# The first channel quarter's modulation in two halves, in one core's hybrid decoder layer

## The chip, the core and the metric

The kernel runs on one core of a Trainium2 chip. The metric is the device time of one execution in microseconds (us), here the median of three runs. The engines are PE (TensorE matmuls), PEld (its weight loads), DVE (VectorE), ACT (ScalarE), POOL (GpSimd) and SP (SyncE, which issues the large loads). Each works through its own program in order, and semaphores tie them together.

## What is computed

One step of a hybrid decoder layer for 256 prompt rows and 32 sample rows (8 sequences of 4), 288 rows in all, D_MODEL = 2048, all in float32.

```
mods = silu(c) @ w_ada + b_ada          # -> shift1, scale1, gate1, shift2, scale2, gate2
h    = RMSNorm(x; g_pre1) * (1 + scale1) + shift1
h @ w_in -> q, k, v, forget logits, u, B, C, gA, gB
A    = forgetting attention(q, k, v)    # 16 heads x 64
y    = B * conv3_causal(C * u)
m    = (sigmoid(gA) * (A @ w_oa) + sigmoid(gB) * (y @ w_ob)) @ w_o
x    = x + gate1 * RMSNorm(m; g_post1)
x    = x + gate2 * RMSNorm(SwiGLU(RMSNorm(x; g_pre2) * (1 + scale2) + shift2); g_post2)
```

There are 9 conditioning rows: one for the prompt, 8 for the samples. `w_ada` is 2048 x 12288.

## The kernel before

**Layout and precision.** Activations lie transposed: 16 tiles of 128 channels, each with 288 columns (`NT`). Every float32 product of weights and activations is three matmuls in the fast 32-bit format: the weights are split into `w_hi` (ACT, a cast) and `w_lo` (DVE, `raw - w_hi`), the activations into `a_hi` and `a_lo`. One load into `raw` brings 4 channel tiles (`SK`) by 512 weight columns (`SN`), 1 MiB. There are 4 `raw` buffers (`RAW`) and 2 split buffers (`SPLIT`). `product` multiplies one load: for each of 4 column tiles of 128 (`mt`, one PSUM bank each) it runs 4 channel tiles x 3 matmuls, 48 in all.

**Rounds.** The first stage computes u, C and B. It goes channel quarter by channel quarter (4 channel tiles each), so that it can start before the whole of h is there. A quarter has five rounds, one for each of five groups of 512 columns (`CUT` = 5, `round_cols`). Round n has column group n % 5 and quarter n // 5; there are 20. In quarter 0 ACT copies the result out of the banks into `acc_half` (`first_round`), in later quarters DVE adds it there (`later_round`). A round can use a bank only when its previous content is out (`bank_turn`), and its split buffer only when the round two before it is multiplied (`mm_turn`).

**Visits.** scale1 and shift1 of a channel quarter are 512 columns of `w_ada` each. One visit brings one of them: four loads of 1 MiB, one per quarter of the summed dimension, into the ring `ada`, then `ada_slot` for each (4 matmuls of 128 x 512 float32 in four column strips of PE, into bank 4), a copy to `ada_sb` (ACT, `copy_ada`), four transposes into bank 5 (PE, `ada_transpose`), and a reduction into `mods` (DVE, `add_ada`). Visit 2c is the scale of quarter c, visit 2c + 1 its shift. A slot of the ring is loaded again when the visit before has multiplied it (`ada_turn`). Visits 0 and 1 stand before round 0, visit 2 behind round 1, visit 3 behind round 3, 4 and 5 behind rounds 5 and 7, 6 and 7 behind rounds 10 and 12. The transposes of a visit stand inside the round behind it, between two column tiles (`between`).

**From a visit to h.** Behind the scale: `prepare_scale` (DVE: bias, `modA`, x * scale * rstd into `xn`). Behind the shift: `prepare_shift` (DVE), `split_h` (ACT: `a_hi`, in two pieces of 2 channel tiles), `h_lo` (DVE: `a_lo`, likewise). A quarter's first round waits for its `h_lo` (`act_lo`).

**Order.** The order on every engine is written out by hand. SP issues the loads of rounds and visits in one fixed sequence (`load_first`, `load_rounds`), and each issue waits until its buffer is free. While SP waits, all loads behind it in its program wait too. Fillers (`keep_warm`: matmuls of 256 columns whose result is not used) stand in the lead-in where PE would have nothing to do.

## Time and profile before

| | |
|---|---|
| median of 3 runs | 1842.09 us |
| lowest, highest | 1840.67, 1842.49 us |
| the profiled execution's own time | 1839.91 us |
| its span, first to last instruction | 1838.1 us |
| PE busy in the span | 1806.4 us, 98% |
| PE, first product of round 0 | 44.57 us |
| PE, first product of quarter 1 | 86.93 us |
| DVE busy, ACT busy | 875.1 us (48%), 704.8 us (38%) |

The page of the profile gives busy times, the costliest groups of instructions by line, and what ended the idle time before them. The timeline merges instructions of one line that follow one another on an engine; an instruction's end there is its result, so the next one often starts before it. "x32" of a visit's matmuls stands for 16 instructions in two records each. SPq rows are the issues of loads, and an issue lasts as long as the queue has no room. The time to landing is counted from the issue.

### The profile page before, as it was taken

The page shows a single profiled execution, that of the slowest core. Times are in us where ns is not written, and L with a number is a line of the kernel's source. Part 1 is how long each engine was busy: PE and PEld are TensorE (multiplying, and loading weights), DVE is VectorE, ACT ScalarE, POOL GpSimd, SP SyncE. Part 2 cuts the span into 40 slices and gives each one's busy share as a digit, 9 for nine tenths or more (in the row PEclk, how much of TensorE's full clock was granted, in tenths as well). Part 3 has the DMA queues.
Part 4 walks back from the last instruction along what each step waited for, and adds up shares of the span by engine and source line. Part 5 has one row for each costly group of instructions (what it writes and reads, how often), then busy time and mean ns, then how long its engine had stood idle before and what let it go on. Part 6 is the DMA issues. An engine that isn't in the chain of part 4 may idle for free.

```text
span 1838.1 us, 31832 instructions
## 1 busy us (share of the span) xinstructions
PE 1806.4 (98%) x13703; PEld 1684.8 (92%) x13703; DVE 875.1 (48%) x1041; ACT 704.8 (38%) x817; POOL 26.7 (1%) x77
## 2 busy tenths in 40 slices
PE   8999999999999999999999999999999999999997
PEld 4889978887589999999969999999999999999996
DVE  4456743334644343453365434444444445566565
ACT  3423222334643333343354233333333334555453
POOL 0001000010000000000000000000000000000000
PEclk9999999999999999999999999999999999999999
DMA  9987878864665555449847464444444445544441
GB/s 344 386 320 247 301 266 331 319 252 167 230 207 161 164 170 169 160 144 352 318 170 252 138 251 161 160 162 169 170 161 160 160 162 173 169 161 161 162 160 52
DMA packets 189591, 382.37 MB, mean 208 GB/s; under 512 B 8789, under 2 KB 9261, under 8 KB 189199
## 3 DMA queue, kind: packets, MB, share of 16 engines
q1 hardware_dynamic: 185744, 378.04, 58.8%
q0 software_dynamic: 1328, 2.58, 0.4%
q8 instruction: 74, 1.21, 0.3%
q10 hardware_dynamic: 2424, 0.37, 0.2%
q14 instruction: 21, 0.17, 0.0%
HBM read 376.15 MB, written 4.81 MB: 207 GB/s over the span
## 4 chain that ended last, share of the span: by engine, by line
PE 95%; DVE 2%; ACT 1%; DMA 1%; issue 1%; SPq 0%; DVEq 0%; ACTq 0%
PE bank L566 29%; PE bank L568 28%; PE bank L567 28%; PE bank L576 4%; PE bank L771 1%; PE bank L905 1%; DMA ada<-in_w_ada 1%; DMA x_rows<-in_x_sample 1%; PE bank L584 1%; PE bank L874 0%; PE bank L622 0%; PE bank L824 0%; DVE xT L2027 0%; PE bank L841 0%; ACT w_hi L1074 0%
## 5 line engine op out<-in xcount | busy, mean ns | idle before, releaser
L566 PE MATMUL bank<-a_lo,w_hi 128*128 128x288 f32 x3648 | 1085.4, 298 | 5.7 <-DVE a_lo L1642 3.2
L567 PE MATMUL bank<-a_hi,w_hi 128*128 128x288 f32 x3648 | 1076.8, 295 | 0.0
L568 PE MATMUL bank<-a_hi,w_lo 128*128 128x288 f32 x3648 | 1073.0, 294 | 0.0
L1507 DVE TENSOR_TENSOR w_lo<-raw,w_hi 128x2048 fp32r<-128x2048 f32 x244 | 559.3, 2292 | 742.2 <-ACT w_hi L1074 741.4
L1074 ACT CAST w_hi<-raw 128x2048 fp32r<-128x2048 f32 x244 | 465.5, 1908 | 833.7 <-PE bank L568 826.8
L566 PEld LDWEIGHTS bank<-a_lo,w_hi 128*128 128x128 f32 x3648 | 684.1, 188 | 24.1 <-issue 18.0
L568 PEld LDWEIGHTS bank<-a_hi,w_lo 128*128 128x128 f32 x3648 | 687.6, 188 | 0.0
L567 PEld LDWEIGHTS bank<-a_hi,w_hi 128*128 128x128 f32 x3648 | 685.6, 188 | 0.0
L576 PE MATMUL bank<-ada,cT 128*32 128x512 f32 x544 | 63.1, 596 | 2.7 <-DMA ada<-in_w_ada 2.7
L1606 DVE TENSOR_TENSOR a_lo<-hid,a_hi 128x1152 fp32r<-128x1152 f32 x44 | 59.4, 1352 | 12.3 <-ACT a_hi L1104 12.3
L1104 ACT CAST a_hi<-hid 128x1152 fp32r<-128x1152 f32 x44 | 50.8, 1156 | 0.0
L576 PEld LDWEIGHTS bank<-ada,cT 128*32 128x32 f32 x544 | 15.3, 109 | 33.8 <-issue 30.8
L1591 DVE TENSOR_REDUCE mods<-bank 128x36 f32<-128x144 f32 (+1 forms) x24 | 7.3, 305 | 73.7 <-PE bank L584 73.7
L1100 ACT COPY ada_sb<-bank 128x512 f32<-128x512 f32 x24 | 14.0, 585 | 73.1 <-PE bank L576 73.1
L566 PE MATMUL bank<-o_lo,w_hi 128*128 128x288 f32 x128 | 37.9, 296 | 0.0
L566 PE MATMUL bank<-y_lo,w_hi 128*128 128x288 f32 x128 | 37.9, 296 | 0.0
L567 PE MATMUL bank<-o_hi,w_hi 128*128 128x288 f32 x128 | 37.8, 295 | 0.0
L567 PE MATMUL bank<-y_hi,w_hi 128*128 128x288 f32 x128 | 37.8, 295 | 0.0
L568 PE MATMUL bank<-y_hi,w_lo 128*128 128x288 f32 x128 | 37.6, 294 | 0.0
L568 PE MATMUL bank<-o_hi,w_lo 128*128 128x288 f32 x128 | 37.6, 294 | 0.0
L1456 ACT ACTIVATE sg<-bank 128x288 f32<-128x288 f32 x44 | 18.0, 408 | 36.8 <-PE bank L568 36.8
L2090 DVE TENSOR_TENSOR sg<-bank,sg 128x288 f32<-128x288 f32 x44 | 19.0, 454 | 15.3 <-ACT sg L1456 15.3
(290 smaller groups left out, 936.9 us busy)
## 6 DMA issues: line engine op xcount, KB each, us to landing
raw<-in_w_ffn_in SPq DMA_DIRECT2D x88, 1024.0 KB, 4.9
raw<-in_w_in SPq DMA_DIRECT2D x80, 1024.0 KB, 7.2
ada<-in_w_ada SPq DMA_DIRECT2D x68, 1024.0 KB, 9.9
raw<-in_w_ffn_out SPq DMA_DIRECT2D x44, 1024.0 KB, 5.1
ada_o<-in_w_ada SPq DMA_DIRECT2D x26, 1024.0 KB, 9.5
raw<-in_w_o SPq DMA_DIRECT2D x16, 1024.0 KB, 5.6
raw<-in_cache_k SPq DMA_DIRECT2D x16, 512.0 KB, 4.4
raw<-in_cache_v SPq DMA_DIRECT2D x16, 512.0 KB, 4.1
```

The lines of the kernel that those rows point to most:

```text
L566: pe.matmul(acc, w_hi[buf][:, a, cols], lo[:, kt, :], start=first and a == 0, stop=False)
L567: pe.matmul(acc, w_hi[buf][:, a, cols], hi[:, kt, :], start=False, stop=False)
L568: mm = pe.matmul(acc, w_lo[buf][:, a, cols], hi[:, kt, :], start=False, stop=last and a == SK - 1)
L576: mm = pe.matmul(bank[4][32 * a:32 * a + 32, :], cT[:, SK * q + a, :], ring[q % len(ring)][:, a, :], start=q == 0, stop=q == SK - 1, tile_ ...
L584: mm = pe.transpose(bank[5][:, m * P:m * P + P], ada_sb[:, m * P:m * P + P], ident[:, :])
L771: mm = pe.transpose(bank[4 + n % 2][:, f * P:f * P + P], raw[2 * j][:, n, f * P:f * P + P], ident[:, :])
L905: mm = pe.matmul(acc, lhs, rhs, start=blk == 0, stop=blk == 2, tile_position=(0, 32 * c), skip_group_check=True)
L1074: nc.scalar.copy(w_hi[buf][:, :, :], raw[s][:, :, :]).then_inc(hi_done, 1)
L1104: nc.scalar.copy(dst[:, kd:kd + tiles, :], src[:, bass.ds(kt, tiles), :]).then_inc(act_hi, 1)
L1507: tt(w_lo[buf][:, :, :], raw[s][:, :, :], w_hi[buf][:, :, :].bitcast(F32), ALU.subtract).then_inc(raw_turn, 1)
L1606: tt(lo[:, kd:kd + SK, :], src[:, bass.ds(kt, SK), :], hi[:, kd:kd + SK, :].bitcast(F32), ALU.subtract).then_inc(act_lo, 1)
L2090: tt(sg[:, mt, :], bank[mt][:, 0:NT], sg[:, mt, :], ALU.mult).then_inc(bank_turn, 1)
```

## The change

Three things change, all in the first stage.

**Visits of quarter 0.** They come as four visits of 256 columns: scale and shift of channel tiles 0 and 1, then of 2 and 3. A slot's load is 128 x 4 x 256 (512 KB, runs of 1 KB where they were 2 KB). All later visits keep 512 columns and move up by two (`SPARE` = 2): 4 and 5 serve quarter 1, 6 and 7 quarter 2, 8 and 9 quarter 3.

**Rounds of quarter 0.** Four of the five column groups (`EARLY` = 4) are multiplied by two channel tiles at a time: rounds 0 to 3 with tiles 0 and 1, rounds 4 to 7 with tiles 2 and 3, 24 matmuls each, their weights loaded as 128 x 2 x 512 (512 KB). Round 8 is the fifth column group with all four tiles. Quarters 1 to 3 are rounds 9 to 23. DVE adds rounds 4 to 7, ACT copies out 0 to 3 and 8.

**Where the visits stand.** Visit 2 stands behind round 1, visit 3 inside round 2 before its last column tile, visit 4 behind round 7, visit 5 behind round 8 with fillers around its transposes. In quarters 1 and 2 the scale's visit stands behind the second round (it was the first), the shift's behind the fourth (it was the third), with its transposes after the first column tile of the fifth round. SP's sequence of loads follows.

```diff
+    EARLY = 4
-    ROUNDS = CUT * (KT // SK)
+    ROUNDS = EARLY + CUT * (KT // SK)
...
+        def round_of(n):
+            if n < 2 * EARLY:
+                return n % EARLY, HALF * (n // EARLY), HALF
+            return (n - EARLY) % CUT, SK * ((n - EARLY) // CUT), SK
...
             load_first(0)
             load_rounds(0, 1)
             load_first(1)
-            load_rounds(1, 3)
+            load_rounds(1, 4)
             load_first(2)
-            load_rounds(3, 6)
             load_first(3)
-            load_rounds(6, 9)
+            load_rounds(4, 8)
             load_first(4)
-            load_rounds(9, 11)
+            load_rounds(8, 10)
             load_first(5)
+            load_rounds(10, 11)
+            load_first(6)
             load_rounds(11, 13)
-            load_first(6)
-            load_rounds(13, 15)
             load_first(7)
-            load_rounds(15, ROUNDS)
+            load_rounds(13, 16)
+            load_first(8)
+            load_rounds(16, 18)
+            load_first(9)
+            load_rounds(18, ROUNDS)
...
             round_product(0)
             round_product(1)
-            ada_group(2)
-            round_product(2, 2)
-            round_product(3)
-            ada_group(3)
-            round_product(4, 3)
+            pe.wait_ge(ada_copied, 3)
+            for q in range(SK):
+                early_slot(q, 2)
+            def fourth_visit(mt):
+                if mt == 3:
+                    ada_transpose(2, HALF)
+                    pe.wait_ge(ada_copied, 4)
+                    for q in range(SK):
+                        early_slot(q, 3)
+            round_product(2, None, fourth_visit)
+            def its_transposes(mt):
+                if mt == 1:
+                    ada_transpose(3, HALF)
+            round_product(3, None, its_transposes)
+            for n in range(EARLY, 2 * EARLY):
+                round_product(n)
+            ada_group(4)
+            round_product(2 * EARLY, 4)
+            ada_group(5)
+            keep_warm(1)
+            ada_transpose(5)
+            keep_warm(4)
             for c in (1, 2):
-                round_product(CUT * c)
-                ada_group(2 * c + 2)
-                round_product(CUT * c + 1, 2 * c + 2)
-                round_product(CUT * c + 2)
-                ada_group(2 * c + 3)
-                round_product(CUT * c + 3, 2 * c + 3)
-                round_product(CUT * c + 4)
+                n = EARLY + CUT * c
+                v = 2 * c + 4
+                round_product(n)
+                round_product(n + 1)
+                ada_group(v)
+                round_product(n + 2, v)
+                round_product(n + 3)
+                ada_group(v + 1)
+                def shift_transposes(mt):
+                    if mt == 1:
+                        ada_transpose(v + 1)
+                round_product(n + 4, None, shift_transposes)
```

SP's program, behind the loads of visit 1. Before (L406 is a visit's load, L410 a round's; `ada0` to `ada3` are the ring's slots):

```order
L410 DMA raw1_73<-in_w_in 128x4x512
L410 DMA raw2_74<-in_w_in 128x4x512
L406 DMA ada0_83<-in_w_ada 128x4x512
L406 DMA ada1_84<-in_w_ada 128x4x512
L406 DMA ada2_85<-in_w_ada 128x4x512
L406 DMA ada3_86<-in_w_ada 128x4x512
L410 DMA raw3_75<-in_w_in 128x4x512
L410 DMA raw0_72<-in_w_in 128x4x512
L410 DMA raw1_73<-in_w_in 128x4x512
```

The same place after the change:

```order
L443 DMA raw3_75<-in_w_in 128x2x512
L428 DMA ada0_83<-in_w_ada 128x4x256
L428 DMA ada1_84<-in_w_ada 128x4x256
L428 DMA ada2_85<-in_w_ada 128x4x256
L428 DMA ada3_86<-in_w_ada 128x4x256
L428 DMA ada0_83<-in_w_ada 128x4x256
L428 DMA ada1_84<-in_w_ada 128x4x256
L428 DMA ada2_85<-in_w_ada 128x4x256
L428 DMA ada3_86<-in_w_ada 128x4x256
L443 DMA raw0_72<-in_w_in 128x2x512
```

Two visits now stand one directly behind the other, and the weights of rounds 4 to 7 behind both.

PE's program, at the visit that follows round 1 before the change:

```order
L566 MATMUL bank3<-a_lo_82,w_hi1_78 128x288
L567 MATMUL bank3<-a_hi_81,w_hi1_78 128x288
L568 MATMUL bank3<-a_hi_81,w_lo1_79 128x288
L576 MATMUL bank4<-ada0_83,cT_58 32x512 x4
L576 MATMUL bank4<-ada1_84,cT_58 32x512 x4
L576 MATMUL bank4<-ada2_85,cT_58 32x512 x4
L576 MATMUL bank4<-ada3_86,cT_58 32x512 x4
L566 MATMUL bank0<-a_lo_82,w_hi0_76 128x288
```

And at visit 3 inside round 2 after it (L612 are the transposes of visit 2, L603 the slots):

```order
L595 MATMUL bank2<-a_hi_81,w_lo0_77 128x288
L612 MATMUL bank5<-ident_49,ada_sb_69 128x128 x2
L603 MATMUL bank4<-ada0_83,cT_58 32x256 x4
L603 MATMUL bank4<-ada1_84,cT_58 32x256 x4
L603 MATMUL bank4<-ada2_85,cT_58 32x256 x4
L603 MATMUL bank4<-ada3_86,cT_58 32x256 x4
L593 MATMUL bank3<-a_lo_82,w_hi0_76 128x288
```

A visit that stood between two rounds now stands between two column tiles of one round, with half the columns.

ACT's program in quarter 1, from the copy of the scale's visit to the shift's `a_hi`. Before (the casts are `w_hi` of rounds 7, 8 and 9):

```order
L1100 COPY ada_sb_69<-bank4 128x512
L1074 CAST w_hi1_78<-raw3_75 128x2048
L1074 CAST w_hi0_76<-raw0_72 128x2048
L1100 COPY ada_sb_69<-bank4 128x512
L1074 CAST w_hi1_78<-raw1_73 128x2048
L1111 ACTIVATE a_hi_81<-xn0_100,mods_55 128x256 x2
```

After (the casts behind the first copy are `w_hi` of rounds 13 and 14):

```order
L1163 COPY ada_sb_69<-bank4 128x512
L1137 CAST w_hi1_78<-raw1_73 128x2048
L1137 CAST w_hi0_76<-raw2_74 128x2048
L1163 COPY ada_sb_69<-bank4 128x512
L1177 ACTIVATE a_hi_81<-xn0_100,mods_55 128x256 x2
```

The shift's copy stood behind the casts of the quarter's third and fourth rounds, and stands behind those of its fifth and of the next quarter's first.

## Rows read from the trace of the kernel before

**Rows 1.** The page, part 1: busy time, share of the span, instructions.

```profile
PE 1806.4 (98%) x13703; PEld 1684.8 (92%) x13703; DVE 875.1 (48%) x1041; ACT 704.8 (38%) x817; POOL 26.7 (1%) x77
```

**Rows 2.** Timeline of PE, 23 to 45 us: start, length, line, what, idle before.

```profile
23.74 1.07 PE L576 MATMUL bank<-ada,cT 128*32 128x512 f32 x8
...
28.08 0.94 PE L657 MATMUL bank<-diag,ones 128*128 128x128 f32 x6
...
38.07 1.07 PE L576 MATMUL bank<-ada,cT 128*32 128x512 f32 x8 [0.58 <-DMA ada<-in_w_ada]
...
40.33 2.75 PE L595 MATMUL bank<-ones 128*128 128x256 f32 x12
44.57 0.40 PE L566 MATMUL bank<-a_lo,w_hi 128*128 128x288 f32 x1 [1.49 <-DVE a_lo L1642]
```

**Rows 3.** The same timeline, DVE and ACT.

```profile
25.77 0.28 DVE L1540 COPY st_T<-bank 128x128 f32<-128x128 f32 x1
...
39.20 0.59 ACT L1100 COPY ada_sb<-bank 128x512 f32<-128x512 f32 x1 [9.89 <-PE bank L576]
...
41.43 0.91 ACT L1111 ACTIVATE a_hi<-xn,mods 128x256 fp32r<-128x256 f32 x2 [1.65 <-DVE xn L1631]
...
42.38 0.90 ACT L1111 ACTIVATE a_hi<-xn,mods 128x256 fp32r<-128x256 f32 x2
```

**Rows 4.** Timeline of PE, 57 to 138 us: four visits and quarter 1's first product.

```profile
57.56 3.64 PE L576 MATMUL bank<-ada,cT 128*32 128x512 f32 x32
...
86.93 0.40 PE L566 MATMUL bank<-a_lo,w_hi 128*128 128x288 f32 x1 [1.71 <-DVE a_lo L1642]
...
93.52 3.64 PE L576 MATMUL bank<-ada,cT 128*32 128x512 f32 x32
...
110.51 3.64 PE L576 MATMUL bank<-ada,cT 128*32 128x512 f32 x32
...
133.91 3.64 PE L576 MATMUL bank<-ada,cT 128*32 128x512 f32 x32
```

**Rows 5.** The page, part 5: group | busy us, mean ns | idle before, releaser.

```profile
L1507 DVE TENSOR_TENSOR w_lo<-raw,w_hi 128x2048 fp32r<-128x2048 f32 x244 | 559.3, 2292 | 742.2 <-ACT w_hi L1074 741.4
L1074 ACT CAST w_hi<-raw 128x2048 fp32r<-128x2048 f32 x244 | 465.5, 1908 | 833.7 <-PE bank L568 826.8
```

**Rows 6.** Groups by line, 44 to 130 us.

```profile
L1659 DVE TENSOR_TENSOR acc_C<-bank,acc_C 128x288 f32<-128x288 f32 x8 | 3.3, 453 | 1.8 <-PE bank L568 1.8
L1143 ACT COPY acc_C<-bank 128x288 f32<-128x288 f32 x8 | 3.1, 396 | 3.8 <-PE bank L568 3.8
```

**Rows 7.** Timeline of SP's issues, 135 to 186 us.

```profile
135.03 2.94 SPq L406 DMA_DIRECT2D ada<-in_w_ada  x4
138.02 47.46 SPq L410 DMA_DIRECT2D raw<-in_w_in  x8
```

**Rows 8.** DMA issues at 135.03 and at 138.02: KB, us from issue to landing.

```profile
ada<-in_w_ada SPq DMA_DIRECT2D x1, 1024.0 KB, 4.9
...
raw<-in_w_in SPq DMA_DIRECT2D x1, 1024.0 KB, 14.2
```

**Rows 9.** Stretches: length, busy time of five engines, granted clock, DMA share, GB/s.

```profile
30.00:40.00 10.00, 8.23 (x47) 3.14 (x48) 4.37 (x7) 0.59 (x1) 0.00 (x0) 1.00 1.04 387
130.00:136.00 6.00, 6.00 (x50) 4.42 (x53) 3.46 (x5) 0.00 (x0) 0.00 (x0) 1.00 0.05 18
```

**Rows 10.** The page, part 3: packets, MB, share of 16 engines' span.

```profile
q1 hardware_dynamic: 185744, 378.04, 58.8%
...
q10 hardware_dynamic: 2424, 0.37, 0.2%
```

**Rows 11.** Stretches and PE's timeline where the granted clock fell.

```profile
508.00:512.00 4.00, 2.63 (x12) 1.47 (x13) 2.99 (x4) 1.79 (x7) 0.00 (x0) 0.50 1.05 402
512.00:516.00 4.00, 4.00 (x32) 3.20 (x36) 0.11 (x1) 0.00 (x0) 0.00 (x0) 0.66 0.16 60
...
508.69 1.12 PE L851 MATMUL bank<-pT_p,v_rows 128*64 128x256 f32 x4 [2.34 <-ACT pT_p L1266]
```

326 lines of the change are left out of this document (195 added, 131 removed).

## The prediction

> **What bounds the kernel now.** I read the busy shares first: PE works 98% of the span [rows 1], so whatever PE waits for, or is given on top, moves the end. All weights are split and multiplied at one pace: two rounds of 48 matmuls start at 44.57 and are followed by the visit at 57.56 [rows 2, 4], 6.4 us a round and 0.1 between. Behind the four channel quarters of the first rounds the change moves nothing, so the question is when PE gets through them.
>
> Next the start. Before the first product at 44.57 PE does filler and small work. What ends last there is the second visit: its last slot starts at 38.07 when its megabyte has landed, then come copy, transposes, shift, the two splits, and PE starts 5.43 us after the slot's end at 39.14 [rows 2, 3]. The queue is full: 387 GB/s between 30 and 40 [rows 9], 2.7 us for each 1024 KB. The change goes for this wait.
>
> Then quarter 0: PE waits once more, 1.71 us before 86.93, where quarter 1 begins [rows 4]. From there visits start at 93.52 and 110.51, 16.99 apart, which is 3.64 for the four slots, two rounds of 6.4 and one set of transposes (0.4), with no wait [rows 4]. So the ground to compare is: first product, start of quarter 1, waits in quarters 1 and 2.
>
> **Term 1, first product: 44.6 becomes 33.6.** Four slots take 3.64 [rows 4], 0.91 each. A slot of 256 columns lies between 0.45 (half) and 0.91 (nothing saved); I take 0.48, since six fillers of 256 columns took 2.75 [rows 2], 0.43 each, so columns set the time. Two slots stand ahead of 23.74: PE is there at 22.9. Slots 2 and 3 and two fillers end by 24.7; the copies of the vectors (ended 26.05 [rows 3]) move to 25.2; two transposes and the six small matmuls (0.94 [rows 2]) end at 26.4. Four half slots with three fillers between: 29.6. Are their loads there? Slots 2 and 3 of the ring come free at 23.4 and 23.9, when the queue has run dry. A load into an idle queue landed after 4.9 us [rows 8]; with half the bytes I say 3.8, and 1.6 for the next (below): 27.2 and 28.8, wanted at 28.2 and 29.1. Just in time. The chain of 5.43 loses 0.2 in the copy, 0.2 in the transposes, 0.95 since only one of the two pieces (starts 41.43 and 42.38 [rows 3]) is needed, 0.1 elsewhere: 4.0. First product at 33.6, 11.0 us earlier.
>
> **A half load.** It is 512 packets of 1 KB. A 2 KB packet took 0.588 x 16 x 1838.1 / 185744 = 93 ns, a packet of the small queue (153 B on average) 0.002 x 16 x 1838.1 / 2424 = 24 ns [rows 10]; the line between them gives 56 ns at 1 KB, 0.60 of a large one, so 1.63 us for 512 KB. Bounds: 1.36 (half) and 2.7 (a packet costs what it did). A rule of the Trainium skill speaks against the change here: the page "DMA: Bandwidth & Descriptors", section "Bandwidth", wants loads of at least 1 MiB for three quarters of the peak, and its section "Anatomy of one DMA — SWDGE (gpsimd) path" has a fixed 2.0 us for each DMA beside bytes at 436 GB/s. In a full queue the trace does not show the fixed part (387 GB/s with 1024 KB loads [rows 9]); into an idle queue it does, 4.9 measured against the page's 4.4 for 1024 KB. By the page each half load into an idle queue would land after 3.2 and the wait below would be 0.6 shorter.
>
> **Term 2, first product to quarter 1: 42.4 becomes 55.7.** The rounds are the same 240 matmuls, 32.0. What is new, in order:
> - Rounds 0 and 1 (3.2 each) end at 40.0, the third visit's half slots at 41.95. ScalarE evicts round 1 only behind the copy of this visit, and round 2 needs that bank: copy 0.37 (512 columns took 0.59 [rows 3], 288 took 0.40 [rows 6]), eviction 0.40: round 2 starts at 42.85, 0.9 of wait.
> - The fourth visit stands inside round 2. Its loads wait for the slots that the third frees, 40.5 to 42.0, and the queue has run dry: SyncE issued the third visit by 30, and rounds 4 to 7 stand behind the fourth in its program. They land at 44.3, 46.0, 47.6, 49.2. PE is there at 45.55 and leaves at 49.7 instead of 47.5: 2.2.
> - Round 2 ends at 50.5, transposes stand after one column tile of round 3: 51.6. Round 3 ends at 54.0. Reduce, bias, shift on VectorE to 52.6, ScalarE's a_hi 0.95, and only behind it w_hi of round 4 (1.03 for half of 1908 ns), then w_lo (1.23 for half of 2292 ns [rows 5]): 56.0. Wait 2.0.
> - Rounds 4 to 7 end at 68.8 (per round VectorE has 1.2 of split and 4 x 0.4 of adding [rows 6], under 3.2: hidden). Visit 4 to 72.4, 0.4 for an eviction queued behind the split of round 8, round 8 with transposes to 79.7, visit 5 with 0.4 wait for its last load (issued from 69.8: 4.9 + 3 x 2.7 = 82.8) to 83.8.
> - Nothing stands between visit 5 and quarter 1 but fillers. The whole chain of 5.4 [rows 2, 3] is open: 89.2. Before, it lay behind a round and showed as 1.71.
>
> So quarter 1 begins at 89.3, against 86.93: **+2.3**. Of the 11.0 gained, 4.4 go to half slots and transposes that now stand behind the first product, 5.9 to the waits, and 3.0 more to the chain that lies open.
>
> **Term 3, quarters 1 and 2: +1.8 to +3.2 each.** Visits 7 and 9 are loaded ahead of the weights of rounds 13 and 14, and 18 and 19. Count from G, the start of visit 6. Its first slot is free and the load issued at G+1.1 (133.91 is such a start in the trace [rows 4], 135.03 the issue [rows 7]). The queue is empty then, as before 135.03 (18 GB/s [rows 9]). The four loads and then raw 13 go through: at 2.7 each behind the first 4.9, raw 13 lands at G+16.9; in the one such case of the trace the fifth load, issued at 138.02, took 14.2 [rows 7, 8] and landed at 152.2, G+18.3. PE has visit, round, round, visit to do, 16.99 + 3.64 = G+20.6, and the two splits need 4.25 (1.91 and 2.29 [rows 5]): raw 13 must land by G+16.4. Late by 0.5 or by 1.9. What hangs behind: ScalarE copies visit 7 only behind the split of round 14, VectorE adds round 12 behind the split of 13 and reduces visit 7 behind the split of 14; the bank costs 0.4, quarter 2's h_lo ends 12.0 after raw 13 (0.4 late), its first bank 0.4. Sum 1.75 or 3.15 a quarter, twice (visits 7 and 9). Before, the weights of the same rounds (9 and 10 then) stood ahead of the visit. I take one of each: **+4.9**.
>
> Sum: 2.3 + 4.9 = +7.2. From the profiled 1838.1 (its own time 1839.9) to 1847.1; on the median of 1842.1, 2.2 above that profile, **1849.3**.
>
> **Rivals.**
> 1. The quarters do not wait: raw 13 lands by G+16.4. The chain has 0.8 of slack then, and only term 2 is left: 1844.4. For it: 0.5 us decides. Against: the trace's one case is 1.4 later, not earlier.
> 2. Faster. The waits in quarter 0 do not come (0.9 + 2.2 + 2.0 + 0.8), because loads land sooner than an idle queue has shown, and the open chain is short. With half slots and transposes still paid, 11.0 - 4.4 = 6.6 is the most, 3.6 with the chain as priced: 1835.5 to 1838.5. It decides where all the waits, the open chain and term 3 together stay under 6.6 - 3.7 = 2.9. Against: two of them are order on ScalarE, not loads.
> 3. The clock falls. PE idled 2.34 before 508.69 and its granted clock was 0.50 and 0.66 in the next 8 us [rows 11], 6.7 us at 1.2 GHz, 3.4 lost. Here PE idles 2.0 before round 4 and 2.6 before quarter 1, fillers between. The 1.71 before 86.93 cost no clock. Price 3.4: 1852.7. The Trainium skill ("TensorE: Matmul & The Clock Gate", "What's actually happening") says throttled is the default and activity releases it; the trace agrees with 0.50 behind an idle stretch.
> 4. Small packets cost what large ones do: 16 half loads at 2.7 delay visits 1 and 3 above all, some 13 on top: 1862.
>
> **How the numbers follow.** Forecast (1847 to 1851.5) 0.54; rival 1: 0.21; rival 2: 0.06; rival 3: 0.14; rival 4: 0.05. A measurement can tell 0.2%, 3.7 us, from no change: 1838.4 to 1845.8. Rival 1 lies within it (0.20, a little of it above); rival 2 below (0.06); the rest above (0.74). The range takes rival 1 and rival 3 with a slow load in each quarter: 1844 to 1855. A slot at its upper bound of 0.91 would add 4.5, and lies inside.
>
> **What would show it.** First product near 33.6; gaps of PE of about 2 inside round 2, 2 before round 4, 2.6 behind the fillers after visit 5; quarter 1 at 89; a wait on w_lo before round 13 and round 18. Right in sign but wrong in mechanism, if quarter 1 begins before 87. Wrong, if PE runs the quarters unbroken from 34 on.

## The result, and the profile after

The changed kernel took 1857.26 us (median of 4 runs, 1855.13 to 1857.91) against 1842.29 for the kernel before (4 runs, 1840.67 to 1843.31): ratio 1.008, 95% interval 1.0068 to 1.0092. It is slower by 15.0 us. The prediction said slower, but at 1849.3 with 1844 to 1855 as its range: the sign was right, the size was half of what came (7.2 of 15.0 us), and the time lies outside the range. The profiled execution took 1857.5 us, its span is 1855.9 (before: 1838.1), so between the two profiles there are 17.8 us to find.

The page, part 1, busy time by engine, beside [rows 1]: of the 17.8 us PE is busy 9.2 longer and idle 8.6 longer (40.3 in place of 31.7).

```profile
PE 1815.6 (98%) x13769; PEld 1693.3 (91%) x13769; DVE 882.6 (48%) x1069; ACT 705.6 (38%) x823; POOL 26.0 (1%) x77
```

PE's timeline of the changed kernel (start, length, line, operation, in brackets the idle time before it and what ended it), the rows that answer to [rows 2] and [rows 4]. L593 is a product's first matmul, L603 a slot of a visit, L612 a transpose, L623 a filler:

```profile
34.76 0.40 PE L593 MATMUL bank<-a_lo,w_hi 128*128 128x288 f32 x1 [0.40 <-DVE a_lo L1727]
...
44.17 0.37 PE L593 MATMUL bank<-a_lo,w_hi 128*128 128x288 f32 x1 [0.88 <-ACT acc_C L1217]
50.17 0.64 PE L603 MATMUL bank<-ada,cT 128*32 128x256 f32 x8 [2.15 <-DMA ada<-in_w_ada]
51.63 0.64 PE L603 MATMUL bank<-ada,cT 128*32 128x256 f32 x8 [0.83 <-DMA ada<-in_w_ada]
58.59 0.37 PE L593 MATMUL bank<-a_lo,w_hi 128*128 128x288 f32 x1 [1.78 <-DVE w_lo L1746]
...
87.69 1.06 PE L603 MATMUL bank<-ada,cT 128*32 128x512 f32 x8 [1.26 <-DMA ada<-in_w_ada]
88.69 0.70 PE L623 MATMUL bank<-ones 128*128 128x256 f32 x2
89.47 0.66 PE L612 MATMUL bank<-ident,ada_sb 128*128 128x128 f32 x4
89.96 1.89 PE L623 MATMUL bank<-ones 128*128 128x256 f32 x8
94.20 0.61 PE L593 MATMUL bank<-a_lo,w_hi 128*128 128x288 f32 x1 [2.35 <-DVE a_lo L1727]
...
131.96 0.58 PE L593 MATMUL bank<-a_lo,w_hi 128*128 128x288 f32 x1 [2.77 <-DVE acc_u L1757]
...
176.04 0.58 PE L593 MATMUL bank<-a_lo,w_hi 128*128 128x288 f32 x1 [2.38 <-DVE acc_u L1757]
...
229.79 3.64 PE L603 MATMUL bank<-ada,cT 128*32 128x512 f32 x32
```

The first product starts at 34.76 in place of 44.57: 9.8 us gained. Quarter 1 starts at 94.20 in place of 86.93: those 9.8 and 7.3 more are gone by then. The visit behind the first rounds (that of B1, the next tile of weights) starts at 229.79; in the kernel before it is this row, so 16.6 of the 17.8 us are there by then:

```profile
213.23 3.64 PE L576 MATMUL bank<-ada,cT 128*32 128x512 f32 x32
```

The rows at 94.20, 131.96 and 176.04 show a second thing. A first matmul took 0.40 at 34.76 and takes 0.61 and 0.58 there: half clock. Four stretches of the changed kernel (length, busy time and instructions of PE, PEld, DVE, ACT and POOL, granted clock, DMA share, GB/s), of which the first begins 1.1 us behind the row at 58.59:

```profile
59.70:63.10 3.40, 3.40 (x17) 3.40 (x16) 2.10 (x4) 0.00 (x0) 0.00 (x0) 0.51 1.04 387
93.90:97.30 3.40, 3.10 (x13) 3.10 (x14) 2.54 (x3) 0.94 (x1) 0.00 (x0) 0.50 1.04 383
...
131.40:134.80 3.40, 2.84 (x12) 2.87 (x13) 3.40 (x6) 0.92 (x2) 0.00 (x0) 0.50 1.04 386
175.80:179.20 3.40, 3.16 (x13) 3.17 (x14) 3.39 (x5) 0.60 (x2) 0.00 (x0) 0.50 1.04 374
```

The eighth column is the granted clock: 0.50 is 1.2 GHz in place of 2.4, called half clock below. Half of PE's busy time in these stretches is lost: 1.7, 1.55, 1.4 and 1.6, together 6.3 us. In the kernel before the first 507 us hold no such stretch.

Behind the two waits in the quarters (before rounds 13 and 18) stand the raw loads; raw 13 is the load of round 13's weights. SyncE's issues and the DMA issues of the stretch 109 to 114 us (columns as in [rows 7] and [rows 8]; the median of the four slot loads of visit 7 is 9.5):

```profile
109.68 2.94 SPq L416 DMA_DIRECT2D ada<-in_w_ada  x4
112.67 8.26 SPq L420 DMA_DIRECT2D raw<-in_w_in  x3
```

```profile
raw<-in_w_in SPq DMA_DIRECT2D x1, 1024.0 KB, 14.5
```

Raw 13 was issued at 112.67 and landed at 127.2. With G = 108.56 (the start of visit 6) that is G+18.6: the later of the two values that the prediction carried (16.9 and 18.3). Raw 18 was issued at 157.15 and took 14.1: G+18.2, with G = 153.03. PE's releaser is acc_u, the addition that frees the bank; it stands on VectorE right behind the w_lo of round 13, as the prediction had it.

The queue was not slow while raw 13 was under way. This is the stretch from just before the first of visit 7's loads to its landing:

```profile
109.00:127.17 18.17, 18.17 (x148) 14.59 (x144) 8.78 (x19) 2.21 (x2) 0.00 (x0) 1.00 0.93 338
```

338 GB/s over 18.17 us are 6.1 MB; visit 7's four loads and raw 13 are 5.2. So 0.9 MB of the loads issued behind raw 13 had moved before its last packets: a load counts as landed when its last packet is in, and by then the queue was partly working on later ones. Had the bytes gone strictly in order, raw 13 would have been there some 2.3 us earlier (an estimate, 0.9 MB at the 387 GB/s of a full queue), at about G+16.3, where the prediction put the limit at G+16.4.

**The ledger.** Profile against profile, 17.8 = 16.6 before the B1 visit + 1.2 behind it. A stretch at half clock near the end is 10.2 us long in place of 6.8; that the 1.2 come from it is not shown.

| | before | after | difference | of it half clock |
|---|---|---|---|---|
| first product | 44.57 | 34.76 | -9.8 | |
| first product to quarter 1 | 42.4 | 59.4 | +17.1 | 1.7 |
| quarter 1 to the B1 visit | 126.3 | 135.6 | +9.3 | 4.6 |

### The profile page after: what moved, and what is told of

Its sections match the earlier page's. It is cut to its first block, busy times and chain, and to the rows that moved or that the text cites. A ratio compares the mean times of both kernels' runs of the same rounds, so it can differ in the third digit from the quotient of the medians.

```text
span 1855.9 us, 32027 instructions
## 1 busy us (share of the span) xinstructions
PE 1815.6 (98%) x13769; PEld 1693.3 (91%) x13769; DVE 882.6 (48%) x1069; ACT 705.6 (38%) x823; POOL 26.0 (1%) x77
## 4 chain that ended last, share of the span: by engine, by line
PE 91%; DMA 3%; DVE 3%; ACT 2%; issue 1%; POOL 0%; SPq 0%; DVEq 0%; ACTq 0%; POOLq 0%
PE bank L593 28%; PE bank L595 27%; PE bank L594 27%; PE bank L603 3%; DMA raw<-in_w_in 2%; DMA ada<-in_w_ada 1%; PE bank L834 1%; PE bank L968 1%; DVE w_lo L1586 1%; ACT w_hi L1137 1%; PE bank L623 1%; PE bank L937 0%; PE bank L650 0%; PE bank L612 0%; PE bank L887 0%
## 5 line engine op out<-in xcount | busy, mean ns | idle before, releaser
L593 PE MATMUL bank<-a_lo,w_hi 128*128 128x288 f32 x3648 | 1088.3, 298 | 14.0 <-DVE acc_u L1757 5.1
L1586 DVE TENSOR_TENSOR w_lo<-raw,w_hi 128x2048 fp32r<-128x2048 f32 x240 | 550.0, 2292 | 720.8 <-ACT w_hi L1137 720.1
L1137 ACT CAST w_hi<-raw 128x2048 fp32r<-128x2048 f32 x240 | 457.7, 1907 | 874.8 <-PE bank L595 814.4
L593 PEld LDWEIGHTS bank<-a_lo,w_hi 128*128 128x128 f32 x3648 | 686.4, 188 | 33.2 <-issue 27.3
L603 PE MATMUL bank<-ada,cT 128*32 128x512 f32 (+1 forms) x608 | 64.0, 552 | 4.2 <-DMA ada<-in_w_ada 4.2
L1686 DVE TENSOR_TENSOR a_lo<-hid,a_hi 128x1152 fp32r<-128x1152 f32 x44 | 59.4, 1351 | 12.3 <-ACT a_hi L1167 12.3
L603 PEld LDWEIGHTS bank<-ada,cT 128*32 128x32 f32 x608 | 17.0, 109 | 37.3 <-issue 29.8
L593 PE MATMUL bank<-o_lo,w_hi 128*128 128x288 f32 x128 | 37.9, 296 | 0.0
L593 PE MATMUL bank<-y_lo,w_hi 128*128 128x288 f32 x128 | 37.9, 296 | 0.0
L1163 ACT COPY ada_sb<-bank 128x512 f32<-128x512 f32 (+1 forms) x26 | 14.4, 552 | 48.4 <-PE bank L603 48.4
```

What stands on the lines that cost most here:

```text
L593: pe.matmul(acc, w_hi[buf][:, a, cols], lo[:, kt, :], start=first and a == 0, stop=False)
L603: mm = pe.matmul(bank[4][32 * a:32 * a + 32, 0:cols], cT[:, SK * q + a, :], ring[q % len(ring)][:, a, 0:cols], start=q == 0, stop=q == SK ...
L1137: nc.scalar.copy(w_hi[buf][:, :, :], raw[s][:, :, :]).then_inc(hi_done, 1)
L1586: tt(w_lo[buf][:, :, :], raw[s][:, :, :], w_hi[buf][:, :, :].bitcast(F32), ALU.subtract).then_inc(raw_turn, 1)
L1686: tt(lo[:, kd:kd + SK, :], src[:, bass.ds(kt, SK), :], hi[:, kd:kd + SK, :].bitcast(F32), ALU.subtract).then_inc(act_lo, 1)
```

## The experiments

The theory after the result, A: the change loses in three separable ways. The order of loads in quarters 1 and 2 starves the splits; the four half visits and the open chain behind visit 5 leave holes in quarter 0; and the clock falls behind some of these holes. Rivals: the new order of instructions in the quarters costs by itself; small packets are what slows quarter 0; quarter 0 is bound by bytes, so that a hole mended comes back elsewhere. The kernel before was measured again beside each group of experiments (1842.54, 1841.45, 1841.25 and 1841.66), and each ratio stands against it.

**1. The order of loads in the quarters.** The changed kernel with the raw loads of rounds 11 to 14 and 16 to 19 nearer to the front, so that those of 13, 14, 18 and 19 stand ahead of visits 7 and 9; nothing else differs.

```diff
-            load_rounds(10, 11)
+            load_rounds(10, 13)
             load_first(6)
-            load_rounds(11, 13)
+            load_rounds(13, 15)
             load_first(7)
-            load_rounds(13, 16)
+            load_rounds(15, 18)
             load_first(8)
-            load_rounds(16, 18)
+            load_rounds(18, 20)
             load_first(9)
-            load_rounds(18, ROUNDS)
+            load_rounds(20, ROUNDS)
```

> The changed kernel with one edit: SP's sequence in quarters 1 and 2 issues the weights of rounds 13 and 14 ahead of visit 7, and of 18 and 19 ahead of visit 9 (10 to 12, visit 6, 13 and 14, visit 7, 15 to 17, visit 8, 18 and 19, visit 9). Theory A, the order on SP makes the waits before rounds 13 and 18: the waits of 2.77 and 2.38 us go, and with each its 3.4 us at half clock (1.7 lost); -8 to -9, so 1848.5 to 1849.5. Rival B, the waits come from the order on ACT and DVE (visit 7 is copied behind the split of round 14): they stay, 1856 to 1858.

Measured: 1849.03 (5 runs, 1845.50 to 1850.20), ratio 1.0037 (1.0023 to 1.0051), 8.2 us under the changed kernel, as theory A had it. PE's timeline from 57 us on: every row with an idle time over 0.5, and the B1 visit; and the stretch from 26 us to it:

```profile
57.73 0.38 PE L593 MATMUL bank<-a_lo,w_hi 128*128 128x288 f32 x1 [1.78 <-DVE w_lo L1746]
75.77 0.37 PE L593 MATMUL bank<-a_lo,w_hi 128*128 128x288 f32 x1 [1.44 <-DVE acc_u L1757]
...
92.46 0.40 PE L593 MATMUL bank<-a_lo,w_hi 128*128 128x288 f32 x1 [2.35 <-DVE a_lo L1727]
...
218.74 3.64 PE L603 MATMUL bank<-ada,cT 128*32 128x512 f32 x32
```

```profile
26.00:218.70 192.70, 183.20 (x1412) 157.87 (x1410) 115.39 (x221) 62.66 (x80) 8.77 (x16) 1.00 0.90 320
```

The waits before rounds 13 and 18 are gone, and quarter 1 to the B1 visit takes 126.28 us: exactly the 126.30 of the kernel before. This execution had the full clock in the whole stretch, though the waits of 1.78 and 2.35 stand where the changed kernel's clock fell. It was the fastest of the five, 1845.5 at a mean clock of 0.996; the others took 1847.0 to 1850.2 at 0.994 and 0.993. So the same program loses the clock in one execution and keeps it in another.

**2. The old order of quarters 1 and 2** in the changed kernel, on all engines, with the kernel before's order of loads there:

```diff
                 round_product(n)
-                round_product(n + 1)
                 ada_group(v)
-                round_product(n + 2, v)
-                round_product(n + 3)
+                round_product(n + 1, v)
+                round_product(n + 2)
                 ada_group(v + 1)
...
-                round_product(n + 4, None, shift_transposes)
+                round_product(n + 3, v + 1)
+                round_product(n + 4)
```

> The changed kernel with quarters 1 and 2 ordered as before the change on all engines: the scale's visit behind the first round, the shift's behind the third, transposes in the round behind, and SP's sequence to match. Quarter 0 stays changed. Theory A: the same two waits and their clock falls go, at most one load of visit 6 is late by 1.7 us; 1848.5 to 1850.5. What is left over 1842.3 is then the price of quarter 0 alone, +6 to +8. Rival C, half rounds and small loads of quarter 0 slow the later quarters whatever their order: over 1854.

Measured: 1852.43 (1851.66 to 1853.16), ratio 1.0054 (1.0037 to 1.0070), above what was expected (1848.5 to 1850.5) and below rival C (over 1854). In PE's timeline quarter 1 starts at 93.00, and then visit 6, which is wanted one round earlier than in the new order, waits for its loads:

```profile
104.12 1.06 PE L603 MATMUL bank<-ada,cT 128*32 128x512 f32 x8 [1.14 <-DMA ada<-in_w_ada]
106.83 1.94 PE L603 MATMUL bank<-ada,cT 128*32 128x512 f32 x8 [1.65 <-DMA ada<-in_w_ada]
```

The length of 1.94 for a slot that takes 1.06 is half clock again; this profile has three such stretches of 3.4 us, at 52.0, 92.9 and 106.6. As a test of the order alone this run is spoiled: it traded the late raw loads for a late visit. Experiments 4 and 5 put the question better.

**3. The clock.** The changed kernel with filler products in four of its waits:

```diff
+            keep_warm(4)
             for n in range(EARLY, 2 * EARLY):
                 round_product(n)
...
             ada_transpose(5)
-            keep_warm(4)
+            keep_warm(9)
...
                 ada_group(v + 1)
+                keep_warm(5)
```

> The changed kernel with more fillers where PE waits: 4 before round 4, 9 instead of 4 behind the transposes of visit 5, 5 before rounds 13 and 18, each filler 0.43 us. No wait is shortened. Theory D, PE's idle stretches of 1.8 to 2.8 us are what the clock falls behind: no half-clock stretch in the first 200 us (there were four of 3.4 us), the first product of each round at the same place or earlier by the clock alone; -6.8 at most, so 1850 to 1852.5. Rival E, the clock falls for another reason: four stretches stay, 1856 to 1858.

Measured: 1853.39 (1851.27 to 1854.30), ratio 1.0060 (1.0043 to 1.0076), 3.9 under the changed kernel and 0.9 above the expected range. The raw loads still miss the limit of G+16.4: raw 13 landed at G+17.0, raw 18 at G+18.3. The stretches from the first product (35.62) on show the full clock, where those of the changed kernel show 0.97 and 0.96 (34.7 to 94.2 and 94.2 to 230):

```profile
35.00:93.00 58.00, 53.22 (x414) 42.44 (x413) 28.43 (x59) 23.50 (x43) 0.00 (x0) 1.00 0.93 332
93.00:224.30 131.30, 130.38 (x978) 117.58 (x976) 82.19 (x151) 36.98 (x34) 8.73 (x16) 1.00 0.84 299
```

From the first product to the B1 visit this profile takes 188.7 us (35.62 to 224.32) and the changed kernel's 195.0: 6.3 less, which is what its four falls were read to cost. The execution lost part of it elsewhere. Its clock fell for 3.4 us at 22.9, in the lead-in, and its first product came 0.9 later; and it fell for 3.4 us at 268.6. Fillers compute nothing that is used, and the median is 3.9 us lower with them: at least that much of the loss is clock.

**4. The new order of the quarters alone,** put into the kernel before: PE, ScalarE, VectorE and SyncE as in the changed kernel from quarter 1 on, quarter 0 untouched.

> The kernel before with only the new order of quarters 1 and 2 on all engines (scale's visit behind the second round, shift's behind the fourth, its transposes after the first column tile of the fifth, SP's sequence to match). Quarter 0 stays as before. Theory A: waits of 2.0 to 2.8 us before rounds 9 and 14, each with 3.4 us at half clock; +7 to +9, so 1849.5 to 1851.5. Rival F, the order only hurts where quarter 0 has left the queue late: no waits, 1841.5 to 1843.5.

Measured: 1849.48 (1845.81 to 1852.00), ratio 1.0031 (1.0017 to 1.0045). PE's timeline, and the stretch behind its first row:

```profile
123.71 0.58 PE L566 MATMUL bank<-a_lo,w_hi 128*128 128x288 f32 x1 [2.80 <-DVE acc_u L1667]
167.28 0.37 PE L566 MATMUL bank<-a_lo,w_hi 128*128 128x288 f32 x1 [1.66 <-DVE acc_u L1667]
```

```profile
123.60:127.00 3.40, 3.29 (x14) 3.31 (x15) 3.26 (x4) 0.47 (x1) 0.00 (x0) 0.50 1.04 387
```

One wait of 2.80 with a fall of the clock, one of 1.66 without. The B1 visit starts at 220.35, 7.1 behind the kernel before. Late loads in the quarters are a defect of their own, and cost half of the whole loss (6.9 of 15.0 us against the kernel measured beside each). This profile is the slowest of its five executions, which ran from 1845.81.

**5. The same order with its loads in time,** the kernel of experiment 4 with the repair of experiment 1:

```diff
             load_first(3)
-            load_rounds(6, 7)
+            load_rounds(6, 9)
             load_first(4)
-            load_rounds(7, 9)
+            load_rounds(9, 11)
             load_first(5)
-            load_rounds(9, 12)
+            load_rounds(11, 14)
             load_first(6)
-            load_rounds(12, 14)
+            load_rounds(14, 16)
             load_first(7)
-            load_rounds(14, ROUNDS)
+            load_rounds(16, ROUNDS)
```

> x4_quarters_only (the kernel before with the new order of quarters 1 and 2) with its loads in another order: the third, first and second rounds' splits behind visits 4 to 7 come ahead of the visit's slot loads, raw loads to 8 before visit 4, to 10 before visit 5, to 13 before visit 6, to 15 before visit 7. Theory A: the new order costs only through the two late raw loads. Then no wait over 0.6 us before rounds 9 and 14, the B1 visit within 0.5 us of 213.23, median 1841.5 to 1843. Rival: the new order has a cost of its own (evictions later, chain to a_lo longer) that shows elsewhere: B1 visit 214.5 or later, median over 1844.

Measured: 1842.01 (10 runs, 1839.73 to 1843.54), ratio 1.0001 (0.9991 to 1.0011); the B1 visit starts here, 0.2 from the kernel before:

```profile
213.46 3.64 PE L576 MATMUL bank<-ada,cT 128*32 128x512 f32 x32
```

The deeper modulation costs nothing when its loads are in time. It gains nothing either: quarter 1 to the B1 visit takes 126.3 us in both orders, and in 125.98 of it PE was busy before the change already.

**6. Half visits side by side.** In the changed kernel all four half visits go to columns 0 to 255 of the ring's slots, so each slot load waits for the visit before it. Here visits 1 and 3 go to columns 256 to 511, with semaphores of their own; the order of loads is that of experiment 1.

```diff
                     for q in range(SK):
-                        sp.wait_ge(ada_turn, SK * v + q + 1)
-                        sp.dma_start(ada[q][:, :, 0:SN // 2],
-                                     wv_ada[q, :, :, col:col + SN // 2]).then_inc(ada_full[q], 16)
+                        if v >= SPARE:
+                            sp.wait_ge(ada_turn, SK * (v - 1) + q + 1)
+                        c0 = v % 2 * (SN // 2)
+                        sp.dma_start(ada[q][:, :, c0:c0 + SN // 2],
+                                     wv_ada[q, :, :, col:col + SN // 2]).then_inc((ada_full, ada_right)[v % 2][q], 16)
```

> The changed kernel with the x1_sp_order order of loads, and the four half visits laid side by side: visits 0 and 2 use the left 256 columns of the four ada slots, visits 1 and 3 the right 256, with semaphores of their own, so that visit 1's loads wait for nothing, visit 2's for visit 0's slots and visit 3's for visit 1's. Theory G: the wait of about 3.4 us within visit 3 of the changed kernel (2.1 in x1_sp_order's trace), and part of the time to the first product, come from SyncE standing at a slot that is still in use while the DMA queues run empty. Then the first product starts at 33.3 to 34.2 us (35.05 in x1_sp_order), visit 3 has no idle row over 0.5, the B1 visit starts 2.5 to 4.5 us earlier than x1_sp_order's 218.74, and the median is 1844.5 to 1846.5. Rival H: this stretch is bound by bytes, and a wait that goes from visit 3 comes back at rounds 4 to 9, visit 4 or visit 5: the B1 visit within 1 us of 218.74, median 1848 to 1850.

Measured: 1845.43 (10 runs, 1843.78 to 1847.78), ratio 1.0020 (1.0010 to 1.0029). Against the kernel before measured beside it, that is 4.0 us over, where experiment 1 was 6.5 over: 2.5 better, though the two intervals still overlap. Three stretches of the changed kernel, and behind them the same three of this one:

```profile
36.00:42.00 6.00, 6.00 (x53) 5.61 (x55) 1.23 (x1) 2.41 (x5) 0.00 (x0) 1.00 0.53 164
42.00:44.00 2.00, 1.29 (x24) 0.52 (x16) 0.00 (x0) 0.64 (x3) 0.00 (x0) 1.00 0.35 85
44.00:50.00 6.00, 3.85 (x36) 3.05 (x36) 2.81 (x8) 1.88 (x5) 0.00 (x0) 1.00 1.05 351
```

```profile
36.00:42.00 6.00, 6.00 (x59) 5.49 (x61) 1.23 (x1) 2.15 (x4) 0.00 (x0) 1.00 1.09 351
42.00:44.00 2.00, 1.11 (x21) 0.49 (x14) 0.00 (x0) 0.94 (x4) 0.00 (x0) 1.00 1.05 386
44.00:50.00 6.00, 5.61 (x59) 4.32 (x59) 2.96 (x8) 2.93 (x9) 0.00 (x0) 1.00 0.22 80
```

The queue that ran at 164 and 85 GB/s while SyncE stood at a slot in use now runs at 351 and 386, and PE is busy 5.61 of the 6 us in which visit 3 stands, not 3.85. Visit 3 waits for nothing:

```profile
46.65 1.93 PE L606 MATMUL bank<-ada,cT 128*32 128x256 f32 x32
...
55.40 0.37 PE L596 MATMUL bank<-a_lo,w_hi 128*128 128x288 f32 x1 [1.79 <-DVE w_lo L1751]
...
84.13 1.07 PE L606 MATMUL bank<-ada,cT 128*32 128x512 f32 x8 [0.90 <-DMA ada<-in_w_ada]
...
90.64 0.40 PE L596 MATMUL bank<-a_lo,w_hi 128*128 128x288 f32 x1 [2.35 <-DVE a_lo L1732]
```

The theory behind this run holds for the wait; the median and the row of visit 3 came as it said. Two of its numbers did not. The first product starts at 34.47. From visit 1's first slot (26.31) to it are 8.16 us, and in the changed kernel (26.61 to 34.76) 8.15: the side-by-side slots gained nothing there. And the B1 visit came at 218.45, as late as in experiment 1, because this profile's clock fell twice (3.4 us each, from 56.8 and from 90.9) where experiment 1's had not fallen at all. Experiment 1's profile is the fastest of its executions and this one the slowest of its ten, so the two rows at the B1 visit can't be set against each other; without the fall at 56.8, first product to quarter 1 takes about 54.5 us here (56.17 less 1.7, an estimate) and 57.41 there.

**7. Round 4's wait.** Experiment 6 with ScalarE's and VectorE's splits of round 4 ahead of the second half of the first quarter's channels:

```diff
             first_round(2)
-            split_h(0, 1)
             split_round(4)
+            split_h(0, 1)
```

> x5_halves_side_by_side and round 4's split ahead: ScalarE splits round 4 before it makes the second half of the first channel tile group, VectorE before it adds visit 3. Theory I: the 1.8 us that TensorE waits before round 4 in every kernel so far is round 4's w_lo queued behind h_lo on VectorE; then the wait is under 0.8, and the median is 1.0 to 1.8 us under x5's. Rival J: behind w_lo stands a_lo of the same tiles, which ends as late; the row before round 4 only changes its releaser, wait 1.3 to 2.4, and the median is within 0.6 us of x5's.

Measured: 1846.44 (1843.93 to 1848.55), ratio 1.0027 (1.0017 to 1.0037): no gain, as rival J had it, though 1.0 and not 0.6 at most from experiment 6; the two intervals overlap. PE's row before round 4:

```profile
55.71 0.40 PE L596 MATMUL bank<-a_lo,w_hi 128*128 128x288 f32 x1 [1.68 <-DVE a_lo L1732]
```

1.79 has become 1.68, and its releaser w_lo has become a_lo. Two chains end together in this place, and putting one ahead leaves PE waiting for the other.

**8. Small packets alone.** The kernel before, with each slot load of visits 0 to 7 as two DMAs of 256 columns, so that the same bytes go as packets of 1 KB, in twice as many DMAs:

```diff
-                    load_ada(SK * g + q, q, wv_ada[q, :, :, col:col + SN])
+                    sp.wait_ge(ada_turn, SK * g + q + 1)
+                    for c0, full in ((0, ada_left), (SN // 2, ada_full)):
+                        sp.dma_start(ada[q][:, :, c0:c0 + SN // 2],
+                                     wv_ada[q, :, :, col + c0:col + c0 + SN // 2]).then_inc(full[q], 16)
```

> The kernel before, with one edit: each slot load of visits 0 to 7 is two DMAs of 256 columns into the two halves of the slot, so the same bytes go in packets of half the size and in twice as many DMAs. Theory K: a packet of 1 KB costs a little over half of one of 2 KB (346 to 360 GB/s against 387 to 396 in the traces), 0.29 us per slot: first product 1.5 to 3 us later than 44.6, B1 visit 2 to 6 us later than 213.23, median 1844 to 1849. Rival L (rival 4 of the prediction, small packets cost like large): every slot load takes twice its time, first product over 8 us later, median over 1856. Rival M (only bytes count): first product within 0.5 us, median 1841.5 to 1843.3.

Measured: 1845.00 (10 runs, 1843.42 to 1847.96), ratio 1.0021 (1.0011 to 1.0030). The stretch 26 to 36 us of this kernel, and behind it that of the kernel before:

```profile
26.00:36.00 10.00, 7.32 (x38) 3.23 (x40) 5.95 (x14) 2.48 (x2) 0.00 (x0) 0.83 1.09 353
```

```profile
26.00:36.00 10.00, 7.79 (x52) 3.36 (x44) 5.58 (x12) 2.38 (x2) 0.00 (x0) 1.00 1.04 387
```

353 against 387 GB/s, 9% less. It is the packets and not the size of a DMA: in the changed kernel between 52.0 and 55.5 the queue moved no 1 KB packets, only 2 KB ones, at 394 GB/s, while it was working off the 512 KB loads of rounds 4 to 7. 512 KB in 1 KB packets take 1.49 us in a full queue, where the prediction had 1.63. The first product starts at 47.50 in place of 44.57: the eight slots ahead of it are 8.4 MB, and at 353 in place of 387 GB/s they take 2.1 us longer. The 0.83 is a fall of the clock in this stretch (3.4 us from 32.6, behind a wait of 2.56 for a slot's load). The changed kernel sends only half as many bytes in small packets, some 1 us of such delay, and it has that inside the 34.76.

**9. Fillers in the best version.** Experiment 6 with four fillers before round 4 and nine for four behind visit 5's transposes:

```diff
+            keep_warm(4)
             for n in range(EARLY, 2 * EARLY):
                 round_product(n)
...
             ada_transpose(5)
-            keep_warm(4)
+            keep_warm(9)
```

> x5_halves_side_by_side with filler products: four before round 4, and nine in place of four behind visit 5's transposes, both inside waits of TensorE that are there anyhow. Theory D (the clock falls behind waits of 1.8 and 2.35 us, 1.7 us each, as the two stretches of 3.4 us at half clock at 56.8 and 90.9 in x5's trace): no stretch at half clock from 26 to 230 us, the B1 visit at 214.7 to 215.7 (218.45 in x5) and a median of 1842 to 1844 against x5's 1845.4. Rival (the falls are there in some executions only, and the median of x5 holds few of them): the trace shows none either, but the median is within 0.7 us of 1845.4.

Measured: 1844.60 (10 runs, 1843.58 to 1852.49), ratio 1.0022 (1.0011 to 1.0033), 0.8 under experiment 6 and 0.6 above the expected range. Its stretch from 26 us to the B1 visit has the full clock, and PE's rows at quarter 1 and at the B1 visit are these:

```profile
26.00:217.30 191.30, 187.04 (x1430) 161.64 (x1430) 115.57 (x223) 62.93 (x81) 8.77 (x16) 1.00 0.89 315
```

```profile
91.03 0.40 PE L596 MATMUL bank<-a_lo,w_hi 128*128 128x288 f32 x1 [0.19 <-DVE a_lo L1733]
...
217.31 1.06 PE L606 MATMUL bank<-ada,cT 128*32 128x512 f32 x8
```

From its first product (35.48) to the B1 visit are 181.8 us, against 184.0 in experiment 6: 2.2 us back of the 3.4 that the two falls cost there. The B1 visit, expected at 214.7 to 215.7, still came at 217.31: the first product was 1.0 later than experiment 6's, and from it to quarter 1 this profile saves 0.6 where the fall at 56.8 had cost 1.7. In the medians only 0.8 of it is seen, and the intervals overlap, so the gain from fillers in this version is not shown. No version of the change that was run, the next included, beats the kernel before; the nearest is experiment 5, which leaves quarter 0 as it was.

**10. A round behind visit 5.** Experiment 6 with visits 4 and 5 one round earlier each, so that the chain behind visit 5 has a round beside it, as in the kernel before:

```diff
-            for n in range(EARLY, 2 * EARLY):
+            for n in range(EARLY, 2 * EARLY - 1):
                 round_product(n)
             ada_group(4)
-            round_product(2 * EARLY, 4)
+            round_product(2 * EARLY - 1, 4)
             ada_group(5)
-            keep_warm(1)
-            ada_transpose(5)
-            keep_warm(4)
+
+            def fifth_transposes(mt):
+                if mt == 1:
+                    ada_transpose(5)
+
+            round_product(2 * EARLY, None, fifth_transposes)
```

> x5_halves_side_by_side with visits 4 and 5 one round earlier each: visit 4 behind round 6 with its transposes in round 7, visit 5 behind round 7 with its transposes in round 8, so that the chain from visit 5 to quarter 1 (copy, transposes, addition, shift, hi and lo) runs beside a round as it does in the kernel before; the loads of visits 4 and 5 go ahead of one raw load each. Theory N (the open chain behind visit 5 is what is left of the loss: 84.13 + 1.07 to 90.64 = 5.4 us without a product in x5, 2.35 of it idle): quarter 1 starts 2 to 4 us earlier than x5's 90.64, the B1 visit likewise (214.5 to 216.5), and the median is 1841.5 to 1843.5. Rival P (the loads set the pace here; the bytes ahead of visit 5's last slot are the same less one raw load of 2.7 us, while TensorE comes to it a round of 6.6 us earlier): visit 5 waits 4 to 6 us for its slots, quarter 1 at 90 to 92.5, the B1 visit at 217.5 to 220, median 1844.5 to 1847.

Measured: 1846.57 (10 runs, 1844.10 to 1851.25), ratio 1.0028 (1.0018 to 1.0037). PE's rows of visit 5 and of quarter 1, and SyncE's row of visit 5's loads:

```profile
77.28 1.07 PE L606 MATMUL bank<-ada,cT 128*32 128x512 f32 x8 [0.87 <-DMA ada<-in_w_ada]
...
79.99 1.07 PE L606 MATMUL bank<-ada,cT 128*32 128x512 f32 x8 [1.65 <-DMA ada<-in_w_ada]
82.70 1.93 PE L606 MATMUL bank<-ada,cT 128*32 128x512 f32 x8 [1.65 <-DMA ada<-in_w_ada]
...
93.57 0.40 PE L596 MATMUL bank<-a_lo,w_hi 128*128 128x288 f32 x1 [0.33 <-DVE a_lo L1737]
```

```profile
69.07 2.94 SPq L417 DMA_DIRECT2D ada<-in_w_ada  x4
```

The chain is covered: its wait falls from 2.35 to 0.33. In its place visit 5 waits 4.2 us in three pieces for its loads, as rival P said; the median lies in rival P's range too, while quarter 1 comes 1.1 later than its latest value (92.5). They can't be issued before visit 4, which starts at 67.95, gives the slots back one by one, and each megabyte then takes its 2.7 us (the three rows stand 2.71 apart). Visit 5 comes too soon behind visit 4 for one ring of four slots. Quarter 1 starts 57.8 us behind the first product (35.75) in place of 56.2; part of that is clock, which fell at 57.4 and for 6.8 us at 81.3, and also at 23.3 in the lead-in.

**What is left of the loss,** read from experiment 9, whose quarters run as the kernel before's do and whose clock does not fall. First product to quarter 1 takes 55.6 us in place of 42.4. PE is busy 52.2 of them in place of 40.65. In the 11.5 us of extra busy time are the slots of two more half visits (2 x 1.93) and their transposes (2 x 0.38) whose counterparts stood ahead of the first product, and fourteen fillers, 6.4 at the 0.46 each of [rows 2]; idle are 1.7 more. So 13.2 us are paid for a first product that comes 9.1 earlier. The fillers stand in the 5.5 us between the end of visit 5 and quarter 1, and in the 1.8 before round 4. Experiment 10 shows that a round in the first of these holes moves the wait to visit 5's loads.

## Why the prediction was wrong, step by step

**Term 1** (33.6) came at 34.76, and between 34.5 and 35.8 in all versions. The step was right in kind, and 1.2 us too early. The loads, on which the prediction had spent its care ("just in time"), cost nothing: no slot of visit 1 waits, and experiment 6 changed nothing here. The chain behind the last slot was right too: the slot starts at 30.20 and lasts 0.64, so 3.9 us are left to the first product, where the sum had 4.0. What was mis-sized are the four half slots with three fillers between: priced at 3.2 (0.48 and 0.43 each), they took 4.2, the slots starting 1.2 apart (26.61, 27.81, 29.01, 30.20). The 0.43 was read from fillers in a row; one alone between two slots took 0.6, and a half slot 0.57.

**The half load** (1.63 us) measured 1.49 in a full queue, within its bounds; rival 4 (small packets like large ones) is excluded by experiment 8. Into the idle queue, visit 3's first half load was priced at 3.8. DMA issues of visit 3's loads, the first and the last two of them (KB, median us from issue to landing):

```profile
ada<-in_w_ada SPq DMA_DIRECT2D x1, 512.0 KB, 3.7
```

```profile
ada<-in_w_ada SPq DMA_DIRECT2D x2, 512.0 KB, 7.6
```

The first was right. The four should have landed at 44.3, 46.0, 47.6 and 49.2; they were issued from 42.05 on, and the slots of the third and fourth start at 50.17 and 51.63, each released by its load. That is the pattern of [rows 8]: behind a restart of an idle queue, one of the next loads comes later than its bytes explain. The prediction used it for raw 13 and not here. Again the queue as a whole was not slow:

```profile
42.00:50.17 8.17, 5.14 (x61) 3.57 (x53) 2.97 (x8) 2.52 (x6) 0.00 (x0) 1.00 0.88 287
```

By 50.17, when the third half load lets PE go, 2.3 MB had moved, the bytes of four and a half; all but some 20 of the four loads' 2048 packets were in, and packets of rounds 4 to 7 with them. The fourth load let PE go 1.5 us later. PE waits for the last few packets of each load. By the fixed part of each DMA that the Trainium skill names for the gpsimd path ("DMA: Bandwidth & Descriptors", section "Anatomy of one DMA — SWDGE (gpsimd) path") the prediction had worked out 3.2 for the first half load and a shorter wait; the trace shows 3.7 and a longer wait.

**Term 2** (+2.3) came as +7.3. The waits by its own list: round 2 0.88 (said 0.9), visit 3 about 3.4 (2.2), round 4 1.78 (2.0), visit 5's last load 1.26 (0.4), the open chain with its 2.35 as said (5.4). So the 5.0 by which term 2 failed are 1.2 from the first product, 1.2 in visit 3, 0.9 in visit 5 and 1.7 of clock. These five places and their releasers were right. The 0.4 before round 8 did not show and round 4's wait was 0.2 shorter; as much came on top in small steps that no run takes apart.

**Term 3** (+4.9) is 9.3, of which 4.6 are clock and 4.7 the waits and the work behind them. The prediction took "one of each" of 1.75 and 3.15. The mechanism was right, and experiments 1, 4 and 5 show it: with the loads in time the term is zero. That the size without the clock fits so well is partly luck. Both raw loads came at the late value (G+18.6 and G+18.2), for which its own price was 2 x 3.15 = 6.3; the waits were 2.77 and 2.38, and what it had added for quarter 2's first round did not show as a wait.

**The step that failed is the clock,** which the sum put at nothing and left to rival 3. The prediction gave it one fall, 3.4 us and a chance of 0.14. It fell four times in the first 180 us, behind each of four waits from 1.78 to 2.77 us, at 1.4 to 1.7 each: 6.3 of the 10.6 us by which the profiles missed the sum (17.8 against 7.2). The sum is 6.3 clock, 3.3 term 2, 1.2 behind the B1 visit, less 0.2 in term 3. On the medians the miss is smaller, 8.0: the prediction added 2.2 because the profile before lay that far below its median, and the profile after lies 0.2 above its own. Experiment 3 confirms the clock's share, 6.3 in the profile and 3.9 in the median. The prediction argued from one fall and one wait without a fall (1.71 before 86.93), and did not apply the question to the waits that it had itself put before rounds 13 and 18. Some of those were longer than the one that it had seen pass without a fall. A priced wait of 2 us or more ought to have carried 1.5 us more, as a term with a chance of its own for each place, not as one rival for all. The rule that it cited of the Trainium skill ("TensorE: Matmul & The Clock Gate", section "What's actually happening"), that throttled is the default and activity releases it, agrees with all four rows: 0.50 or 0.51 behind an idle stretch each time. Taken alone it does not settle which wait brings a fall: experiment 1's profile passed 1.78 and 2.35 at the full clock.

**Rival 1** (the quarters do not wait) fell, with raw 13 at G+18.6. **Rival 2** (faster) fell too, and stays so when all is repaired: its limit was 2.9 us for waits, open chain and quarters together. Experiment 9 has none of the quarters' part and no fall, and still pays 13.2 for 9.1.

## What to carry to other kernels

When a stage is shortened at the front, add up what moves behind the new starting point and which chain loses its cover: here, in experiment 9, 9.1 us came in, and visits, transposes and the holes of uncovered chains took out 13.2 with every load of the quarters in time and no fall of the clock. An order of instructions and the order of its loads are one edit: the same order cost 7 us with two loads late and nothing with them in time. Price every new TensorE wait of about 2 us twice, once as idle time and once as a possible fall of the clock behind it.
